# The last three token chunks of a hybrid encoder layer: 512, 384 and 160 columns instead of 384, 384 and 288, with the last stores on two queues

## The reference

```python
n2 = rmsnorm(h, g_ffn[l])
h = h + (jax.nn.silu(n2 @ w_ffn_gate[l]) * (n2 @ w_ffn_up[l])) @ w_ffn_down[l]
...
y = rmsnorm(h, g_final)        # x * rsqrt(mean(x * x) + eps) * g, over the 1024 channels
```

## Time and profile before

| | us |
|---|---|
| median of 3 runs (1283.2 to 1284.01) | 1283.77 |
| the profiled execution's own time | 1281.71 |
| its span in the trace | 1279.5 |
| outside the span (1281.71 - 1279.5) | 2.21 |
| PE busy in the span | 1242.8 |
| DVE busy in the span | 690.6 |

### The profile page before, as it was taken

The page is one execution under the profiler, slowest core; times in us unless marked ns, Lnnn a source line. Parts: engine busy times, 40 slices in busy tenths (PEclk is TensorE's granted clock), DMA queues, the critical chain, the costliest instruction groups (busy, mean ns, idle before and its releaser), DMA issues.

```text
span 1279.5 us, 21004 instructions
## 1 busy us (share of the span) xinstructions
PE 1242.8 (97%) x8670; PEld 1233.0 (96%) x8670; DVE 690.6 (54%) x827; ACT 408.6 (32%) x585; POOL 556.5 (43%) x336
## 2 busy tenths in 40 slices
PE   7999999999999999997999999999999999999997
PEld 7999899999999999997999999999999999999997
DVE  6795598828455633268734343434343434343445
ACT  5623311416122223214442423242324242424431
POOL 2312121211221244417974646474747474747731
PEclk9999999999999999998999999999999999999998
DMA  9369522154244531112121211211120212121103
GB/s 322 93 146 173 122 67 89 42 126 148 87 166 151 178 107 34 49 34 66 34 63 38 66 34 44 57 45 55 35 66 34 67 34 67 34 67 34 67 13 123
DMA packets 126289, 104.73 MB, mean 82 GB/s; under 512 B 9568, under 2 KB 112096, under 8 KB 126208
## 3 DMA queue, kind: packets, MB, share of 16 engines
q1 hardware_dynamic: 125056, 103.46, 28.1%
q10 hardware_dynamic: 1152, 0.06, 0.1%
HBM read 82.80 MB, written 17.43 MB: 78 GB/s over the span
## 4 chain that ended last, share of the span: by engine, by line
PE 84%; DVE 8%; issue 3%; POOL 2%; ACT 1%; DMA 1%; SPq 0%; POOLq 0%; DVEq 0%; ACTq 0%
PE psum L567 31%; PE psum L754 29%; PE psum L790 14%; PE psum L826 3%; DVE S L1385 1%; POOL w_lo L1321 1%; PE psum L741 1%; PE psum L585 1%; DVE sc_a L1385 1%; DMA xs<-in_x_turned 1%; DVE sc_b L1385 1%; PE psum L659 1%; PE psum L675 1%; POOL w_lo L1279 1%; PE psum L619 1%
## 5 line engine op out<-in xcount | busy, mean ns | idle before, releaser
L1279 POOL TENSOR_TENSOR w_lo<-stage,w_hi 128x1024 fp32r<-128x1024 f32 (+1 forms) x50 | 120.4, 2409 | 421.9 <-ACT w_hi L888 410.2
L754 PE MATMUL psum<-op_hi,w_hi 128*128 128x264 f32 x1120 | 228.4, 285 | 5.0 <-POOL w_lo L1321 3.2
L754 PE MATMUL psum<-op_hi,w_lo 128*128 128x264 f32 x1120 | 226.5, 283 | 0.0
L1385 DVE TENSOR_TENSOR hT<-psum,hT 128x1056 f32<-128x1056 f32 (+2 forms) x104 | 112.9, 1087 | 149.6 <-PE psum L790 80.8
L754 PEld LDWEIGHTS psum<-op_hi,w_hi 128*128 128x128 f32 x1120 | 173.4, 189 | 5.7 <-POOL w_lo L1321 3.7
L754 PEld LDWEIGHTS psum<-op_hi,w_lo 128*128 128x128 f32 x1120 | 174.0, 189 | 0.0
L567 PE MATMUL psum<-x_hi,w_hi 128*128 128x352 f32 x720 | 155.0, 324 | 1.1 <-DVE UP L1385 0.6
L567 PE MATMUL psum<-x_hi,w_lo 128*128 128x352 f32 x720 | 154.3, 323 | 0.0
L567 PE MATMUL psum<-x_lo,w_hi 128*128 128x352 f32 x720 | 154.3, 323 | 0.0
L754 PE MATMUL psum<-low_a,w_hi 128*128 128x264 f32 x720 | 146.3, 285 | 0.0
L567 PEld LDWEIGHTS psum<-x_hi,w_hi 128*128 128x128 f32 x720 | 121.5, 188 | 2.2 <-issue 1.2
(11 more groups left out here) (262 smaller groups left out, 2257.8 us busy)
## 6 DMA issues: line engine op xcount, KB each, us to landing
stage<-in_w_in SPq DMA_DIRECT2D x22, 512.0 KB, 5.0
stage<-in_w_ffn_up SPq DMA_DIRECT2D x14, 512.0 KB, 3.9
stage<-in_w_ffn_down SPq DMA_DIRECT2D x12, 512.0 KB, 3.8
pair_y<-in_w_ffn_gate SPq DMA_DIRECT2D x12, 512.0 KB, 4.6
stage<-in_w_ffn_gate SPq DMA_DIRECT2D x10, 512.0 KB, 3.7
pair_y<-in_w_ffn_down SPq DMA_DIRECT2D x10, 512.0 KB, 4.1
xs<-in_x_turned SPq DMA_DIRECT2D x8, 528.0 KB, 8.6
mp_scratch<-gate_t SPq DMA_DIRECT2D x8, 528.0 KB, 3.5
```

What stands on the lines that cost most here:

```text
L754: mm = pe.matmul(out[:, b, :], w[:, slot, k * P:(k + 1) * P], x[:, b * HB:(b + 1) * HB], start=(first and k == 0 and step == 0), stop=(k = ...
L1279: pool.tensor_tensor(to[:, slot, 0:cols], stage[:, slot, 0:cols], hi[:, slot, 0:cols], ALU.subtract).then_inc(lo_ready, 1)
L1385: return dve.tensor_tensor(out, a, b, op)
```

## The change

The chunks become 512, 384 and 160 columns, 4, 3 and 2 groups of up to 128 tokens (the last group of all has 32 tokens). The names `TILES` and `tok` carry these counts. The buffer for the squares (`sq_five`) gets five slots of 512 columns at another place, and `diag3` has room for four blocks. Of the last chunk's eight stores SP issues those of tiles 0, 2, 4 and 6, and ACT those of tiles 1, 3, 5 and 7.

```diff
-CHUNKS = ((0, 384), (384, 384), (768, 288))
+CHUNKS = ((0, 512), (512, 384), (896, 160))
+TILES = ((0, 4), (4, 3), (7, 2))
...
-        sq_five = sq[:, :, :].rearrange("p a t -> p (a t)")[:, 0:5 * 384].rearrange("p (j c) -> p j c", j=5)
+        _, sq_five = overlay(("pad33", [P, hg_at + 8 * T], F32), ("sq_five", [P, 5, 512], F32))
-        _, diag3 = overlay(("pad23", [P, 4 * T], F32), ("diag3", [P, 3, P], F32))
+        _, diag3 = overlay(("pad23", [P, 4 * T], F32), ("diag3", [P, 4, P], F32))
...
             for i in range(3 * KD):
                 n, (c0, c) = i % KD, CHUNKS[i // KD]
+                if i > 2 * KD and n % 2:
+                    continue
                 sp.wait_ge(y_scaled, i + 1)
                 sp.dma_start(t_out["y"][n * P:(n + 1) * P, c0:c0 + c], chunk(hT, i)).then_inc(y_stored, 16)
...
-                    for j in range(3):
-                        t = tok(3 * b + j)
-                        mm = pe.matmul(aux[0:t, 0, 3 * b + j:3 * b + j + 1], src[:, j * P:j * P + t], ones[:, 0:1],
+                    for j in range(nt):
+                        t = tok(t0 + j)
+                        mm = pe.matmul(aux[0:t, 0, t0 + j:t0 + j + 1], src[:, j * P:j * P + t], ones[:, 0:1],
...
-                for j in range(3):
-                    t = tok(3 * b + j)
+                t0, nt = TILES[b]
+                for j in range(nt):
+                    t = tok(t0 + j)
                     mm = pe.matmul(aux[:, 1, j * P:j * P + t], ones[0:t, :], diag3[0:t, j, 0:t], start=True, stop=True)
...
             chunk_root(2)
+            c0, c = CHUNKS[2]
+            for n in range(1, KD, 2):
+                act.wait_ge(y_scaled, 2 * KD + n + 1)
+                act.dma_start(t_out["y"][n * P:(n + 1) * P, c0:c0 + c], hT[:, n, c0:c0 + c]).then_inc(y_stored, 16)
```

More of the change, by code:

```diff
@@ L832, in chunk_squares @@
                 c0, c = CHUNKS[b]
-                pe.matmul(aux[:, 0, 3 * b:3 * b + 3], ones[:, :], zeros[:, 0:3], start=True, stop=False, skip_group_check=True)
+                t0, nt = TILES[b]
+                pe.matmul(aux[:, 0, t0:t0 + nt], ones[:, :], zeros[:, 0:nt], start=True, stop=False, skip_group_check=True)
                 for n in (5, 6, 7):
@@ L1255, in chunk_root @@
                 act.wait_ge(ms_ready, 3 + b)
-                cols = slice(3 * b, 3 * b + 3)
+                cols = slice(TILES[b][0], sum(TILES[b]))
                 act.activation(ss[:, 1, cols], ss[:, 0, cols], ACT.Sqrt).then_inc(root_ready, 1)
@@ L1408, in inverse_root @@
                 then(tt_(ss[:, 2, c], ss[:, 2, c], ss[:, 3, c], MUL))
-                tt_(scaled[:, :, :], ident[:, :].unsqueeze(1).to_broadcast([P, w, P]),
+                tt_(scaled[:, 0:w, :], ident[:, :].unsqueeze(1).to_broadcast([P, w, P]),
                     ss[:, 2, c].unsqueeze(2).to_broadcast([P, w, P]), MUL).then_inc(diag_ready, 1)
@@ L1919, in chunk_rstd @@
                 dve.wait_ge(ss_turned, 2 + b)
-                inverse_root(3 + b, aux[:, 0, 3 * b:3 * b + 3], diag3, slice(3 * b, 3 * b + 3))
+                t0, nt = TILES[b]
+                inverse_root(3 + b, aux[:, 0, t0:t0 + nt], diag3, slice(t0, t0 + nt))
             def scale_last(i):
```

## The result

The changed kernel takes 1287.83 us (median of 13 runs, 1286.26 to 1296.56), the kernel before 1283.77 on the same chip (13 runs, 1282.79 to 1285.43). The medians lie 4.1 us apart. The ratio is 1.0041 with an interval of 1.0032 to 1.0051; it follows the means, which lie 5.2 us apart because two of the 13 runs took 1294.61 and 1296.56. By either the kernel is slower, by 0.4%; the forecast was 1284.6 with a range up to 1287.2, so it was wrong. The profiled execution took 1287.29 us, of it 1285.1 span; before's took 1281.71 and 1279.5.

What follows compares the result with a forecast made beforehand. PE (84%) and the tail behind its last dense matmul were taken to bound the kernel; nine steps summed to +0.86 us on the 1283.77 median, giving 1284.6, range 1281.9 to 1287.2.

Steps and rivals of the forecast that it cites:

- step 4: Chunk 2's 96 matmuls at 160 columns come every 0.111 us, the weight load's pace: -2.09 us; no new wait.
- rival B: PE's clock falls to half inside chunk 2's 96 matmuls: +3.5 to +13 us, time 1288 to 1298; 7%.
- no change: Whole kernel: a measured time from 1281.2 to 1286.3 us counts as the same as before; 73%.
- steps 7 to 9: Tail: last rows -0.40 us, last scalings -1.07, store lag on two queues -0.36, landing -0.10.
- Steps 1 to 6: Chunk 0 at 512 columns +4.79 us, fourth group +0.88, chunk 1 0, chunk 2 -2.09, last sums -0.66, diagonals -0.13.
- VectorE's thin cover: In chunk 2 VectorE's add and two scalings take 1.30 us a tile beside PE's 1.33, so it just keeps up.
- Rival A: Chunk 2: no weight-load floor, 160 columns take 0.074 us, VectorE sets the pace; -1.3 us, time 1283.3; 10%.
- rival D: Chunk 0: wide matmuls cheaper per column, 512 columns take 0.228 or 0.213 us; -0.3 to -1.6 us; 8%.
- Step 7: Last rows: two of four wide records go, priced at 0.112 to 0.25 us each; -0.40 us taken.
- Steps 8 and 9: Last eight scalings -1.07 us; last stores on two queues -0.36 by removing SP's lag, landing -0.10.
- rival C: Last stores: ACT's issues are slow, +1.8 us at 1.0 us an issue, time 1286.4; 10%.
- step 9: Last stores: two queues cut the lag to about 0.03 us (-0.36), landing -0.10; on SP alone lag over 1.3.

Runs made afterwards that it cites:

- after_sp: Changed kernel with all of the last stores issued by SP, none by ACT: 1292.37 us, 1.0065 to the kernel before.
- after_wsum_0: Changed kernel with only chunk 0's one-column sums widened to 120 columns of ones: 1287.48 us, 1.0034 to the kernel before.
- after_wsum_01: Changed kernel with the sums of chunks 0 and 1 widened to 120 columns, the last chunk's left at one: 1283.79 us, 1.0003 to the kernel before.
- before_sum4: Kernel before with three more one-column matmuls (six records) in chunk 0's sums, results unused: 1284.38 us, 1.0001.
- wsum_0_wide240: Changed kernel with chunk 0's sums widened to 120 columns and the last chunk's matmuls streaming 240 columns instead of 160: 1284.38 us, 1.001.
- after_wsum: Changed kernel with the one-column sums of every chunk widened to 120 columns: 1283.66 us, 1.0005 to the kernel before.
- after_wsum_1: Changed kernel with only chunk 1's one-column sums widened to 120 columns: 1284.81 us, 1.0007 to the kernel before.
- before_wsum_01: Kernel before with the sums of chunks 0 and 1 widened to 120 columns, the last chunk's unchanged: 1281.95 us, 0.9989.
- before_act: Kernel before with four of its last eight stores issued by ACT: 1282.88 us, 0.9995.
- twin profiles: Profiles of `after_sp` and of the changed kernel with last-chunk matmuls streaming 240 columns (1287.26 us, 1.0029), alike up to 1268 us.

## Why the prediction was wrong

The failed step is **step 4**, and with it the 7% of rival B. The step priced chunk 2 at 96 x (0.111 - 0.1328) = -2.09, at a pace that holds only at the full clock. Its pace was right and its condition was not: behind the one-column sums of chunk 1 the clock falls to half in both profiles of the changed kernel, in `after_sp`'s and in `after_wsum_0`'s, the 160-column matmuls then come at 0.213, and the clock stays down for 6.8 us in the first two, for the rest of PE's work on the chunk in the third and for 3.4 us in the fourth. Between the ratios of the changed kernel (1.0041) and of `after_wsum_01` (1.0003) lie 0.38%, 4.9 us of the mean; of the medians it is 3.5 us (1287.87 - 1283.99 against 1283.79 - 1283.39). That is the price of the clock, and it alone takes the result out of "no change".

The argument against B was that in before's trace the same 2 us of one-column matmuls pass at a granted clock of 1.00. That was one execution, and the stretch read there was the sums themselves, whereas the falls mostly begin 0.3 to 1.7 us behind their end. `before_sum4` has such falls with wide matmuls too. B's place was right and its chance was not. Its mechanism was right in part: the narrow matmuls let a fall last or come back (`wsum_0_wide240`), but with the sums of chunk 1 filled the same 160-column matmuls run at a clock of 1.00 (`after_wsum`, `after_wsum_01`, `after_wsum_1`), so it is the sums that start it. That B's lowest price of +3.5 comes near the profile's is luck: B had all 96 matmuls at 0.147, while here some 26 of them ran at 0.213, and 1.82 + 0.65 + 0.89 = 3.36 us are lost in `x24`, the rows and `x60` against `after_wsum_01`.

Step by step, the middle column from `after_wsum_01` against `before_wsum_01`, where neither clock falls before the last sums are over:

| step | foreseen | clock up | changed kernel's profile |
|---|---|---|---|
| 1 chunk 0 at 512 columns | +4.79 | +4.90 | +4.88 |
| 2 fourth group of sums and rows | +0.88 | +0.89 | +0.89 |
| 3 chunk 1 | 0 | 0.00 | +1.53 |
| 4 chunk 2 | -2.09 | -2.13 | +0.47 |
| 4 rows of chunk 1, clearing matmuls | 0 | +0.10 | +0.75 |
| 5 last sums | -0.66 | -0.67 | -0.67 |
| 6 diagonals | -0.13 | -0.14 | -0.13 |
| 7 last rows | -0.40 | -0.07 | -0.65 |
| 8, 9 scalings, stores, landing | -1.53 | -0.87 | -0.80 |
| sum | +0.86 | +2.01 | +6.27 |

The 2.01 agrees with the 1.84 between that pair's medians. So of the 6.27 in the changed kernel's profile 2.01 is the split's, about 1 us of it by a tail (steps 7 to 9) that gained less than foreseen. The clock adds 1.53 + 2.60 + 0.65 = 4.78, and last rows that happened to be shorter in that execution take 0.58 off. Measured against the kernel before itself the tail's part does not show: `after_wsum_01` is 0.40 us above it, and 0.86 was foreseen. `before_wsum_01` is 1.44 below it, for a reason that stays open, and that makes up the difference.

**Steps 1 to 6** were right where the clock is up. Matmuls of 512 columns came at 0.231 (21 steps from 1217.07 to 1221.93). VectorE's release left 0.33 us of the 1.00 us of the earlier trace rows:

```profile
1216.73 0.50 PE L829 MATMUL psum<-f_hi,w_hi 128*128 128x512 f32 x1 [0.33 <-DVE gs L1394]
...
1217.07 0.39 PE L829 MATMUL psum<-f_lo,w_hi 128*128 128x512 f32 x1
...
1221.93 0.40 PE L829 MATMUL psum<-f_lo,w_hi 128*128 128x512 f32 x1
```

The rule of the Trainium skill (TensorE: Matmul & The Clock Gate, LDWEIGHTS) that a load takes its columns over 1.2 GHz, 107 ns for 128, nearly holds at the full clock, where the 160-column matmuls with such a load came every 0.1115 us; at half the clock they came every 0.213 with the same load. VectorE's thin cover held: its tile took 1.34 us (adds at 1271.52 and 1272.86) against PE's 12 x 0.111 = 1.33. Rival A falls with the same number, rival D with 0.231 at 512 columns.

**Step 7** was mis-sized: the place's mean of 0.25 a record was used for both the records that go and those that stay, yet the four left take 1.26 to 1.37 us in eight of the ten profiles of the new split, nearly what six took. Only -0.07 is saved. The 0.84 in the changed kernel's own profile is one of two exceptions: its clock was still at 1.00 in these four records and fell behind them. Four in 0.84 are 0.21 each at the full clock, so the 0.112 that step 7 took for it does not hold in this place, and half the clock is only a part of why a record is long here.

**Steps 8 and 9**: the eight scalings take 2.42 instead of 3.49 as foreseen. ACT's issues cost what SP's do, so rival C falls (own lines of ACT's stores and of SP's in the kernel after):

```profile
L1280 ACTq DMA_DIRECT2D out_y<-hT x4: 338/339/347, 1280.5 to 1282.3; - x4
...
DMA to landing us min/median/max: 1.7/1.7/2.4
```

```profile
L550 SPq DMA_DIRECT2D out_y<-hT x20: 332/332/356, 1251.5 to 1281.9; - x20
...
DMA to landing us min/median/max: 1.6/1.9/2.1
```

The last issue begins at 1282.31, 0.13 behind the last scaling (1279.76 + 2.42), where it was 0.39 before, so the lag is gone as foreseen. But from that issue to the end of the span it is 2.8 us, where it was 1279.5 - 1277.24 = 2.26 before. The landing, expected 0.1 shorter, is 0.5 longer. That the longest of ACT's landings (2.4) is the last one's is inferred from this interval. `before_act` shows the same: its ACT stores land in 1.8 to 2.3 us, its ratio is 0.9995, and the alternating queues bring nothing that can be measured. On the new split the only test is `after_sp`, slower at 1.0065, and in the ratio the clock's falls blur it. The profiles show it apart from them, in the time from the end of the last rows to the end of the span, where PE does no more work: it is 5.77 us in `after_sp` (last issue at 1294.10, 1.2 us behind the last scaling, where step 9 had over 1.3) and 5.12 to 5.43 in the nine profiles of the new split with two queues. On the old split it is 6.28 and 6.30 with two queues and 6.19 to 6.21 with one, in four profiles. So by the one profile of `after_sp` the second queue saves 0.34 to 0.65 us on the short last stores, and on the long ones it saves nothing.

One sentence ahead of the prediction has to be corrected (that ACT issues no other transfer), and with it the prediction's claim that a store issued by ACT is not in the trace: ACT does issue eight transfers earlier in the program, in the kernel before as well. Its trace of transfers and its timeline have them:

```profile
out_pool<-UP ACTq DMA_DIRECT2D x8, 7.5 KB, 1.5
```

```profile
202.69 0.39 ACTq L1049 DMA_DIRECT2D out_pool<-UP  x1
```

The eight issues take 0.34 to 0.51 us. Read in time, they would have left little of rival C.

**What stays open.** Why the clock falls behind these sums in one execution and not in the next is not settled, nor why the falls behind chunk 0's sums, which cost 1.53 us in the changed kernel's profile, hardly show in the medians (`after_wsum_1` against `after_wsum_01`: 1.0007 and 1.0003, intervals overlapping). `before_wsum_01` is the best version of all, by 0.11%; no profile of the kernel before shows a fall that it takes away, so that gain is measured but not explained. Falls in other executions are a likely reason: in that session those of the kernel before go from 1280.84 us at a mean granted clock of 0.995 to 1285.25 at 0.991, those of `before_wsum_01` from 1280.45 at 0.995 to 1283.38 at 0.993. But only the profiles tell where a fall stands.

## What to carry to other kernels

A pace read at the full clock is a price only as long as the clock stays up: before short matmuls are placed behind a run of one-column ones, price the stretch at half the clock as well and give that case a real chance, because one undisturbed profile does not exclude it. Extra columns on the one-column sums, whose pace the weight load sets, cost 0.1 us a sum and kept the clock up here; at the very end, where the result is awaited, they cost 0.8 us. To compare two versions, look also at how the same stretch ahead of the change ran in both profiles. And before an operation is called absent, list it by engine over the whole program, not over the stretch under study.

## What the runs showed of the hardware

- The granted clock can fall to half while PE is busy without a gap: in the changed kernel PE worked without idle time from 1216.73 us on, and the clock fell at about 1242.4. What came just before, 1238.75 to 1241.43, were one-column matmuls. Behind 18 such matmuls at 541 to 543 us it fell in eight of 16 profiles and stayed at 1.00 in the other eight.
- Width at the same pace matters: in the twin profiles, 240 columns and 160 columns both take 0.112 us at the full clock, and both 0.213 at half of it, but there the one was back after 3.4 us and the other not to the end. It does not decide each execution: in `after_wsum_0`'s profile 160 columns were back after 3.4 us too.
- The time at half differs by form: 384 columns take 0.32 us instead of 0.175 (nine steps from 1242.46 to 1245.34), 160 columns 0.213 instead of 0.111.
- A weight load hides 120 columns nearly whole: 18 such matmuls took 2.11 us against 2.01 with one column, 24 took 2.78 against 2.68. Where VectorE then waits for the result, 12 took 2.13 against 1.32.
